# Expert tiles in halves of 512 KB, and the second group's gather split around the first job's last pair of up tiles

## What is computed

```python
def moe_ffn(h, w_router, router_bias, w_up, w_down):
    ...
    _, e_idx = lax.top_k(jnp.where(e_keep, sel, -jnp.inf), TOP_K)
    ...
    def expert_block(args):
        xb, e = args
        gate, up = jnp.split(jnp.matmul(xb, w_up[e]), 2, axis=-1)
        return jnp.matmul(jax.nn.silu(gate) * up, w_down[e])
    ...
    out = jnp.zeros((T + 1, D), h.dtype).at[slot_tok].add(ys * slot_w[:, None].astype(ys.dtype))
```

## Time and profile before

| | us |
|---|---|
| median of three runs | 1462.78 |
| lowest, highest | 1461.36, 1464.81 |
| the profiled execution | 1461.82 |
| its span on the core | 1460.1 |
| TensorE busy | 1426.5 (98%) |
| VectorE, ScalarE busy | 915.8 (63%), 704.7 (48%) |
| moved by DMA | 333.78 MB, 229 GB/s over the span |

### The profile page before, as it was taken

How to read it: one execution, slowest core, us unless ns; L and a number is a source line. 1 busy time by engine, 2 the same in 40 slices (tenths; PEclk the granted TensorE clock), 3 DMA queues, 4 the chain that set the end, 5 groups by cost and what they waited for, 6 DMA issues and landing times.

```text
span 1460.1 us, 20759 instructions
## 1 busy us (share of the span) xinstructions
PE 1426.5 (98%) x8400; PEld 1162.2 (80%) x8400; DVE 915.8 (63%) x1505; ACT 704.7 (48%) x1169; POOL 51.7 (4%) x116
## 2 busy tenths in 40 slices
PE   8999999999999999999999999998999999999995
PEld 7888888888888988889898988888899997445441
DVE  7666578766676765567668666668989685121123
ACT  7455456454554644545755545445546553112211
POOL 0000000000000000000022000001000030000000
PEclk9999999999999999999999999999999999999998
DMA  8754554565555555444345755543554379999997
GB/s 345 283 197 173 200 204 145 202 231 177 198 182 193 202 195 205 177 155 177 131 150 211 252 177 198 191 173 137 174 184 143 137 305 405 376 409 421 419 421 288
DMA packets 50198, 333.78 MB, mean 229 GB/s; under 512 B 5808, under 2 KB 6064, under 8 KB 12208
## 3 DMA queue, kind: packets, MB, share of 16 engines
q1 hardware_dynamic: 48512, 322.55, 58.8%
q10 hardware_dynamic: 1584, 9.83, 1.8%
HBM read 331.31 MB, written 1.05 MB: 228 GB/s over the span
## 4 chain that ended last, share of the span: by engine, by line
PE 89%; DVE 4%; ACT 2%; POOL 2%; DMA 1%; SPq 1%; issue 1%; DVEq 0%; POOLq 0%; ACTq 0%
PE psw L603 55%; PE psy L603 31%; PE psw L606 2%; DVE wlo L1927 1%; SPq L2871 1%; DMA hold<-in_we 1%; ACT whi L1360 1%; POOL r L2790 0%; DVE x L2019 0%; DMA ar<-in_xT 0%; DVE xs L1936 0%; DVE x L2032 0%; ACT gb L1482 0%; DVE r L2001 0%; POOL rstd L2748 0%
## 5 line engine op out<-in xcount | busy, mean ns | idle before, releaser
L603 PE MATMUL psw<-xs,whi 128*128 128x512 f32 (+2 forms) x2160 | 648.1, 365 | 6.4 <-DVE wlo L1927 6.4
L1927 DVE TENSOR_TENSOR wlo<-raw,whi 128x1024 fp32r<-128x1024 f32 (+4 forms) x415 | 477.3, 1194 | 75.0 <-ACT whi L1360 69.9
L603 PE MATMUL psw<-xs,wlo 128*128 128x256 f32 x1848 | 483.4, 280 | 0.1
L603 PEld LDWEIGHTS psw<-xs,whi 128*128 128x128 f32 (+1 forms) x2160 | 374.2, 188 | 61.4 <-DVE wlo L1927 6.4
L1360 ACT ACTIVATE whi<-raw 128x1024 fp32r<-128x1024 f32 (+4 forms) x415 | 402.3, 1024 | 7.6 <-PE psy L603 5.2
L603 PEld LDWEIGHTS psw<-xs,wlo 128*128 128x128 f32 x1848 | 348.9, 189 | 17.6 <-DVE wlo L1927 0.6
L1360 ACT ACTIVATE hf<-psw 128x256 f32<-128x256 f32 x90 | 33.9, 383 | 211.7 <-PE psw L603 211.7
L1972 DVE TENSOR_TENSOR hf<-hf,psw 128x256 f32<-128x256 f32 x82 | 34.0, 420 | 146.0 <-ACT hf L1360 146.0
L1360 ACT ACTIVATE ar<-psw 128x256 f32<-128x256 f32 (+2 forms) x141 | 60.1, 430 | 125.9 <-PE psw L603 121.9
L603 PE MATMUL psy<-whi,hhi 128*128 128x512 f32 x352 | 111.2, 390 | 0.0
L603 PE MATMUL psy<-whi,hlo 128*128 128x512 f32 x352 | 111.0, 389 | 0.0
(11 more groups left out here) (347 smaller groups left out, 1790.7 us busy)
## 6 DMA issues: line engine op xcount, KB each, us to landing
raw<-in_ws SPq DMA_DIRECT2D x189, 1024.0 KB, 4.8
hold<-in_we SPq DMA_DIRECT2D x47, 1024.0 KB, 11.0
raw<-in_we SPq DMA_DIRECT2D x22, 1024.0 KB, 10.4
ar<-in_we SPq DMA_DIRECT2D x20, 1024.0 KB, 12.2
gb<-in_ln ACTq DMA_DIRECT2D x7, 1024.0 KB, 5.2
raw<-in_ws SPq DMA_DIRECT2D x9, 768.0 KB, 4.2
raw<-in_ws SPq DMA_DIRECT2D x4, 672.0 KB, 3.9
raw<-in_ws SPq DMA_DIRECT2D x8, 256.0 KB, 6.8
```

Of the source, the lines that this page charges most:

```text
L603: return e.matmul(o, l, rr, start=start, stop=stop)
L1927: e.tensor_tensor(wlo[i % NS][:, c0:c1], raw_t[slot[i]][:, c0:c1], whi[i % NS][:, c0:c1].bitcast(f32), ALU.subtract).then_inc(*made.up((i, ...
```

## The change

Each tile is loaded as two DMAs of 1024 columns (512 KB, 4 KB a partition), each with a semaphore of its own. `up` waits for the first half before its first block and for the second before its second, `down` before blocks 0 and 2. TensorE signals each half as used on its own, in the middle and at the end of `up` and `down`, and the load of a half waits for the same half of the tile before it in the slot. SyncE's order is first half, second half, next tile. For tiles 96 to 99 the first 512 KB stay one DMA. `gather(1)` is cut in two: q = 0, 1 before up(0, 3), q = 2, 3 behind it.

```diff
-        slot_in = [Signal(sem(f"s_slot{i}"), 16) for i in range(WSLOTS + len(ONCE))]
+        slot_in = [Signal(sem(f"s_slot{i}"), 16) for i in range(2 * (WSLOTS + len(ONCE)))]
...
+                def landed(n, j, h):
+                    for q in job_columns(n):
+                        i = enumber[v][n, q, j]
+                        need.wait_ge(*slot_in[2 * i_slot(v, i) + h].at("we", v, i, h))
...
-                def gather(G):
+                def gather(G, qs=range(4)):
...
                     for k in (2 * j, 2 * j + 1):
+                        landed(n, j, k % 2)
                         for z in range(2):
                             for p0, p1, w in ws:
                                 ins = mm(out[z][p0:p1, :], xes[group_of(n) % 2][:, k, c0 + p0:c0 + p1], w[:, k % 2, 512 * z:512 * z + 512], k == 0, k == 7)
-                    ins.then_inc(*s.pe.up(("used", v, n, j), *([("up", v, n)] if j == 3 else [])))
+                        ins.then_inc(*s.pe.up(("used", v, n, j, k % 2), *([("up", v, n)] if j == 3 and k % 2 else [])))
...
                     for k in range(4):
+                        if k % 2 == 0 and not (halved(v, n, j) and k):
+                            landed(n, j, k // 2)
...
                             ins = mm(b[p0:p1, :], hTb[:, n % 2, k, p0:p1], w[:, k, :], k == 0, k == 3)
-                    ins.then_inc(*s.pe.up(("bank", ("ey", v, n, i)), ("used", v, n, j)))
+                        if k == 1:
+                            ins.then_inc(*s.pe.up(("used", v, n, j, 0)))
+                    ins.then_inc(*s.pe.up(("bank", ("ey", v, n, i)), ("used", v, n, j, 1)))
...
                 up(0, 2)
+                gather(1, (0, 1))
                 up(0, 3)
-                gather(1)
+                gather(1, (2, 3))
...
+                def given_back(h):
+                    if turn_of.get(g, 0) >= WSLOTS:
+                        v_, i_ = esequence[ring[turn_of[g] - WSLOTS]]
+                        need.wait_ge(*(over if v_ else main).pe.at("used", v_, *[etiles[v_][i_][m] for m in (0, 2)], h))
+
                 if late is not None:
+                    given_back(1)
...
                 elif turn_of[g] >= WSLOTS:
-                    v_, i_ = esequence[ring[turn_of[g] - WSLOTS]]
-                    need.wait_ge(*(over if v_ else main).pe.at("used", v_, *[etiles[v_][i_][m] for m in (0, 2)]))
+                    given_back(0)
...
-                if halved(v, n, j):
-                    e.dma_start(wslots[at][:, 0:LATE[0]], src[:, 0:LATE[0]]).then_inc(*slot_in[at].up(("we", v, i)))
-                else:
-                    e.dma_start(wslots[at], src).then_inc(*slot_in[at].up(("we", v, i)))
+                for h in range(1 if halved(v, n, j) else 2):
+                    if h:
+                        given_back(1)
+                    e.dma_start(wslots[at][:, D * h:D * h + D], src[:, D * h:D * h + D]).then_inc(*slot_in[2 * at + h].up(("we", v, i, h)))
```

More of the change, by code:

```diff
@@ L1147, in gate_part @@
                 i = enumber[0]["gate", 0, c]
-                need.wait_ge(*slot_in[i_slot(0, i)].at("we", 0, i))
+                for h in range(2):
+                    need.wait_ge(*slot_in[2 * i_slot(0, i) + h].at("we", 0, i, h))
                 w = blocks(wslots[i_slot(0, i)], T)
@@ L1154, in gate_part @@
                 if t:
-                    ins.then_inc(*pe.up(("bank", ("pleg", c)), ("used", 0, "gate", c)))
+                    ins.then_inc(*pe.up(("bank", ("pleg", c)), ("used", 0, "gate", c, 0), ("used", 0, "gate", c, 1)))
             turned(7, 0)
@@ L1196, in job @@
                     return JOBS * v + n
+                def landed(n, j, h):
+                    for q in job_columns(n):
+                        i = enumber[v][n, q, j]
+                        need.wait_ge(*slot_in[2 * i_slot(v, i) + h].at("we", v, i, h))
                 def weights_in(n, q, j, width=D):
-                    i = enumber[v][n, q, j]
-                    need.wait_ge(*slot_in[i_slot(v, i)].at("we", v, i))
-                    return blocks(wslots[i_slot(v, i)], width)
-                def gather(G):
+                    return blocks(wslots[i_slot(v, enumber[v][n, q, j])], width)
+                def gather(G, qs=range(4)):
                     need.wait_ge(*s.dve.at("pick", v, G))
@@ L1207, in gather @@
                     w_ = 128 * len(group_jobs(G))
-                    for q in range(4):
+                    for q in qs:
                         b = bank("gather", v, G, q)
@@ L1855, in take @@
                     if (v, n, i) == (0, 0, 0):
-                        need.wait_ge(*pe.at("used", 0, 0, 5))
+                        need.wait_ge(*pe.at("used", 0, 0, 5, 1))
                     copy(y_hi[:, 512 * i:512 * i + 512], place["ey", v, n, i][:, :]).then_inc(*s.act.up(("yhi", v, n, i)))
@@ L2944, in sync @@
             n, _, j = etiles[0][ONCE[3]]
-            need.wait_ge(*pe.at("used", 0, n, j))
+            need.wait_ge(*pe.at("used", 0, n, j, 1))
             e.dma_start(gbv, A["ln"][8:9, :].broadcast_to((128, 2 * D))).then_inc(*last_in.up(("gb", 8)))
```

## The result

| | before | after |
|---|---|---|
| median of 10 runs each, same chip | 1462.64 us (1460.81 to 1464.81) | 1468.33 us (1465.43 to 1471.70) |
| profiled execution: time, span | 1461.82, 1460.1 us | 1466.92, 1465.2 us |
| busy share of TensorE, VectorE, ScalarE | 98, 63, 48% | 97, 62, 48% |

The ratio after to before is 1.0037 [1.003, 1.0045]: **the change makes the kernel slower by 0.37%**, 5.7 us by the medians. The prediction was 1463.9 us with a range to 1467.5. The time is outside it, and on the side of the slower rival (1466.6), 1.7 us beyond that too.

A forecast was written before the change was run, and what follows sets the result against it. The prediction took the last load's landing plus 13.2 us as the end. Packets +3.1, recovered holes -2.3 and TensorE waits +0.3 made +1.1 us: median from 1462.78 to 1463.9 us, range 1459.8 to 1467.5.

The forecast's parts named there:

- slower rival: Rival for the expert loads: holes stay and packets cost, tile 44 at 1307.5 us or later, about 1466.6 us; chance 24%.
- What bounds the kernel: End of the experts' part: the last 256 KB landing plus 13.2 us sets the end, with 6.15 us of TensorE idle.
- The packet term: Loads behind tile 44: 4 KB rows cost 0.06 us more a tile over 51 tiles, +3.1 us (2.6 to 4.1).
- four loads in a row: Kernel before, tile 95 to first part of tile 99: 512 KB loads landing 1.27 us each, the source of +0.06 us.
- The recovered holes: Tiles 18 to 44: first halves issued earlier fill part of 6.8 us of holes, -2.3 us (0 to -4.3).
- The best case of -4.3: With no hole left from tile 26 on, tile 44 would land at 1304.1 us instead of 1308.4.
- The 2.0 us held back "for both": Taken off the 4.3 us gain for first halves reaching a queue nearly dry and for an engine that fell behind.
- Waits on TensorE: Second set of waits in `up` and `down`, some 12 places ahead of tile 40's release: +0.3 us.
- the gather: gather(1) split around up(0, 3): tile 25's slot free 1.9 us later, cost 0, at worst +0.5 us on TensorE's path.
- Issue: SyncE: twice as many issues, about 1 us a tile, hidden under the 2.5 us a tile takes to move; cost 0.
- The rule of 1 MiB: Rival that a DMA's fixed cost shows in the 92 added loads: some +200 us, near 1670 us; chance 1%.
- The likely case: The sum of the terms with its bounds, nearly all within 2.9 us of no change; chance 62%.

The follow-up runs named there:

- E10: Kernel before with one 1 MB load a tile, but in rows of 4 KB (gate tiles stay at 8 KB), old waits and release: ratio 1.0023.
- E3: The change without the split of the gather: ratio to the kernel before 1.0031.
- E6: The change with expert weights laid out so that each half is one contiguous 512 KB block in memory: ratio to the kernel before 1.0032.
- E4: Kernel before with halves and finer release for tiles 19 to 44 alone, all others whole, gather whole: ratio 1.0002.
- E1: Kernel before with each tile in two loads of 4 KB rows, waited for and released as a whole, gather whole: ratio 1.0043.
- E2: Kernel before, whole tiles, with only gather(1) split around up(0, 3): ratio 1.0004.
- E9: Kernel before with each tile in two loads, even and odd partitions, whole 8 KB rows, waits and release of whole tiles: ratio 1.000.
- E5: Kernel before with each tile in two loads of 64 neighbouring partitions, whole 8 KB rows, waits and release as a whole: ratio 1.1307, 1654.68 us.
- E11: Kernel before with each tile in four loads of 256 KB in 2 KB rows, waits and release of whole tiles: ratio 1.0133.
- E12: Kernel before, whole tiles, with TensorE's order changed so that down(0, 0) comes ahead of half of gather(1): ratio 1.0002.

## Why the prediction was wrong

It was wrong in its time and its side: forecast +1.1 us, measured +5.1 in the profiled execution and +5.7 in the medians. The 4.0 us missing in the profiled execution are 1.8 of holes that weren't recovered, 2.0 behind tile 44, 0.4 behind the last landing, less 0.3 for waits that cost nothing. By its own steps:

- **What bounds the kernel: right.** The last 256 KB decide, the end is their landing plus 13 us, and TensorE's idle time had nothing to give back. The prediction had put its own falsifier there: the last landing moving by over 3 us. It moved by 4.6.
- **The packet term, +3.1 (2.6 to 4.1): right in kind, and its price inside its bounds.** The stretch from tile 44 to 95 is 5.1 us longer. The cadence is 2.562 us a tile instead of 2.485: 51 x 0.077 = 3.9. I took the 0.06 from four loads in a row, though the window of 408 GB/s gave 0.08; the row closer to the thing itself would have been the better. The other 1.2 us are late landings: three in the kernel after (those at 1320.2, 1377.1 and 1425.1 us come 0.71, 0.66 and 0.62 us beyond the cadence), two before (0.34 and 0.21), while the 0.8 us of tile 44 fell just outside the stretch. The term had no such cost; but other kernels with 8 KB rows have up to 1.6 us of it, and E10 has none, so this part of the difference is at least in part the chance of one execution.
- **The recovered holes, -2.3 (0 to -4.3): the step that failed.** Tile 44 came at 1307.9 us, 0.5 us earlier than before, and not at 1305 to 1307; this is the slower rival's own decision point (1307.5 or later). The best case of -4.3 had tile 26's halves move from 1255.2 and 1257.0 us, one behind the other, and its hole closed. The difference of 3.8 us is: the load before tile 19 came 1.8 us late instead of 0.9, and the 26 tiles took 69.1 us instead of 66.2. Of these 2.9 us, 2.8 lie between the landings of tiles 25 and 26 (5.34 us instead of 2.55). The later holes did close, as forecast. What the sum got wrong is the refill: it counted a half that is issued in time as a half that moves at full rate, and the 8 us behind the hole ran at 314 GB/s where 415 had stood. The 2.0 us held back "for both" named the right kind of thing, a queue near its end and an engine that falls behind, and were too few by 1.8. In E3 and E6, whose tile 26 is only 0.8 and 1.0 us beyond the cadence, tile 44 is 1.1 and 2.0 us earlier than before, counted from gather(0). Why the packets are long in the refill stays open. And E4, with no price behind tile 44, ends level with the kernel before.
- **Waits on TensorE, +0.3: nothing of it; the gather, 0: 0.3.** The two terms had each other's value. In E1, E3 and E4 the added waits leave down(0, 0) where it was; in E2 and in the kernel after the split gather moves it by 0.3 us (bound: +0.5). Neither shows in the time. The 0.3 us come from no wait that the view names; what they are wasn't tried.
- **Issue, 0: right.** From 1407 us on SyncE is held at most issues (0.92 us at 1424.93 in the rows above, where 0.33 is usual), and no hole follows. E9 has the same number of issues at a ratio of 1.000.
- **The rule of 1 MiB**, one of the rivals (near 1670 us), didn't come. The Trainium skill (DMA: Bandwidth & Descriptors, "Measured") asks for at least 1 MiB a DMA, from loads that GpSimd issues; in this full queue of SyncE's E9 has 512 KB loads at a ratio of 1.000. The Trainium skill (DMA: Bandwidth & Descriptors, "Why small descriptors are slow") has a fixed overhead for each packet, and the runs agree that the price goes with the packets. The prediction's estimate from it, 0.03 us a tile, was less than half of the 0.077 measured.
- **The slower rival** said what happened: "holes stay, packets cost". It had 24%. Its time, 1466.6, was 1.7 us short, of which 1.2 are the late landings and 0.4 the clock behind the last landing. Its reason for the first part, a queue that runs dry a second time in each pair, isn't what came: the queue ran low once, at tile 26, and the later pairs have no hole.
- **The sum's structure.** The two large terms, +3.1 and -2.3, weren't equally well founded: one was measured in the kernel, the other argued. The likely case should have been the one without the argued term.

## What to carry to other kernels

What a cut load costs on a full queue is the length of its rows (8, 4, 2 KB: 421, 409, 387 GB/s), not the number of loads. A cut by columns, which can release its buffer in halves, shortens the rows; one by alternating partitions (E9) keeps them, but every matmul here reads all 128 partitions, so it releases nothing earlier. Count what leaves earlier in a hole as time won only if the refill behind it moves at full rate, and look at the window behind the hole as well as at the hole. Where loads wait for buffers that a fully busy engine frees, a late landing can be made good later, as that of tile 26 was in four kernels. And where one term of a forecast is measured and the other argued, try the case in which only the first is true.

## What the runs showed of the hardware that wasn't expected

- **Half the partitions, half the rate, if they are neighbours.** 64 neighbouring partitions: 231 GB/s at a DMA share of 1.02 (E5). 64 alternating ones: 421 GB/s (E9).
- **A price per packet of 9 to 12 ns**, between 8 and 2 KB (9.4 to 9.6 by the cadence, 12 by the packets' records), whether its packets belong to one load or four (E10, E11), and whether they lie together in memory or not (E6).
- **A queue that is refilled by two loads a tile as it runs low is slow for some microseconds**: 264 to 391 GB/s over 8 us with two loads a tile, 403 to 414 with one (E12, with a gap of its own: 357), at a share of 0.81 to 1.01.
- **The 16 engines finish one load up to some microseconds apart**: in 1310 to 1410 us 2.5 to 3.3 in the kernel before, 2.0 to 3.2 in the kernel after, 4.5 to 5.0 in E1. Packets of the instruction queue (68 in the span, 1.11 MB, so 16 KB each) take about 1 us and come every 15 to 25 us in all kernels. Some late landings follow such a packet; most such packets are followed by none, so that they are the cause isn't shown.
- **SyncE's issue is itself a wait when the queue is deep**: 0.9 to 2.8 us instead of 0.33. Near the end it is first held with 10 loads (9 MB) under way in the kernel before, 12 (6 MB) in the kernel after, 7 (7 MB) in E10 and only 16 (8 MB) in E9. So neither the number of loads nor their bytes alone decide; what does wasn't tried.
